# Retention and window-attention trunk: who makes the low parts of four sums of y in the recurrent blocks

## Chip, cores, metric

The kernel runs on one core of a Trainium2 chip. The metric is the device time of one execution in microseconds; lower is better. Times given as "median" are over several executions, times in the trace are those of one profiled execution.

## The reference

Input `x` is 2048 tokens by 1024 features, all in float32. Two layers and a norm:

```python
def reference(x, ...):
    h = x
    h = h + retention_layer(rmsnorm(h, ret_norm), ret_w_in, ret_w_out)   # 4 heads, q/k 256, v 512
    kb, vb = shared_kv(h, kv_norm, w_kv)                                 # once, banded
    h = h + swa_sink_layer(rmsnorm(h, swa_norm), swa_w_in, sinks, swa_w_out, kb, vb)
    return rmsnorm(h, final_norm)
```

What matters here is the end of a retention head: `y = o * silu(g)`, 512 tokens by 512 features for each block of tokens and head, times that head's 512 rows of `w_out`, added to the residual stream `h`.

## The kernel before

**Staging.** The 2048 tokens go through in 4 blocks of 512. Each block has four retention heads one after the other, then the window-attention layer ("post"). Five engines run programs of their own that meet at semaphores; each engine takes its instructions in the order in which the program lists them for it. An instruction whose `wait_ge` isn't fulfilled holds everything behind it on its engine. The five are TensorE (PE; its weight loads are listed as PEld), VectorE (DVE), ScalarE (ACT), GpSimd (POOL) and SyncE (SP), which issues nearly all transfers.

**High and low parts.** Every operand of a large matmul is split into a rounded high part (type fp32r) and the remainder, the low part. A product is three matmuls: high by high, high by low, low by high (`three`, L709 to L711). ScalarE makes most high parts, and the low part is `value - high` on another engine.

**The recurrent blocks.** Block 0 uses plain products. In the blocks 1, 2 and 3 the output product of a head, `y @ w_out`, is done by seven half-size products (a Strassen-Winograd scheme). `y` is transposed on TensorE into PSUM as four quarters A11, A12, A21, A22; four sums are made of them: S1 = A21 + A22, S2 = S1 - A11, S3 = A11 - A21, S4 = A12 - S2. The seven left operands are A11, A12, A22, S1, S2, S3, S4. Each product is 12 matmuls of 128x512.

**Two sorts of head.** Heads of block 1 (`one_head`, "slow heads" below) also prepare weight sums for the later blocks. For this GpSimd makes six pieces a head (`comb_piece(at, j)`, j from 0 to 5): four subtractions of raw weights in place (L655) when the raw data have landed, and a rounding (L663) that waits until the low part of the piece before is done. VectorE makes the piece's low part (`comb_less_hi`, L1979). Heads of the blocks 2 and 3 (`fast_head`, "fast heads") use these sums, and GpSimd has little to do in them. There are 4 slow heads and 8 fast ones.

**The end of a head.** TensorE does the products in this order: A22, the last transposes of y (four in a slow head, eight in a fast one), S1, A11, S2, S3, A12, S4. Before each product it waits for its low part (`part_wait`): for the four sums on the semaphore `s_parts_lo`, for the other three on `a_lo`. Products reuse PSUM banks: the S2 product (slow head) needs the A22 product added to `h`, and the S3 product needs `h_add` at 3, which is the two additions behind the S1 product.

ScalarE makes the high parts in the order A22, S1, A11, A12, S3, S2, S4 (`part_hi`, L1406 fast, L1533 slow). GpSimd makes the low parts of the sums in the order S1, S3, S2, S4 (`y_sums_lo`, L676), each as soon as the high part is there. VectorE, before and after:

```python
gate_y(1)                        # L1825 fast, L2096 slow: y = o * silu(g), last quarter
dve.wait_ge(p_mm.sem, at(p_mm, 1))   # the A22 product is done (t4_mm in a fast head)
add_product(2, 2, 0, 1)          # L1852 fast, L2144 slow: adds it to h
y_sum(S3)                        # L1842 fast, L2131 slow; waits for A12's high part
part_lo(A11)                     # L1678
y_sum(S2)
part_lo(A12)
y_sum(S4)
```

Then come, in a slow head, the low part of weight piece 4 (L1979), a wait for the S1 product, and two additions (`add_product`, L2144 or L1852). Behind these, `add_sum` (L1857, L2149) and `grow_sum` (L1861, L2153) take the other products in, each behind the product that it reads. In a slow head piece 5's low part (L1979 again) follows at the very end of the head.

In GpSimd's queue of a slow head, `y_sums_lo` stands between `comb_piece(at, 4)` and `comb_piece(at, 5)`. In the last head of block 1, TensorE goes on with the transposes of `h` (L1134), which wait for nearly all additions to `h`.

Of the kernel before, what the change touches and what calls it, by code (L numbers as in the profile page):

```python
# [32 lines left out]
F32 = mybir.dt.float32  # L33
F32R = mybir.dt.float32r
I32 = mybir.dt.int32
ALU = mybir.AluOpType
# [6 lines left out]
BLOCKS = SEQ // BT  # L43
# [23 lines left out]
A11, A12, A22, S1, S2, S3, S4 = range(7)  # L67
HI_ORDER = (A22, S1, A11, A12, S3, S2, S4)
LO_ORDER = (A22, A11, A12)
SUM_ORDER = (S1, S3, S2, S4)  # L70
# [38 lines left out]
def build(nc, x, x_t, stream, rope_a, rope_b, mask, ident, ret_cols, gains, sinks, fnorm, out):  # L109
    with ExitStack() as ctx:  # L110
# [89 lines left out]
        asum = {k: v.rearrange("p (t n) -> p t n", t=2) for k, v in asum.items()}  # L200
# [388 lines left out]
        def _(pool):  # L589
# [79 lines left out]
                    pool.wait_ge(x_part_hi.sem, at(x_part_hi, n + 1))  # L669
                    pool.tensor_tensor(xpart[a][1], xsum[a], xpart[a][0].bitcast(F32), ALU.subtract).then_inc(x_part_lo.sem, 1)  # L670

            def y_sums_lo(at):

                for n, a in enumerate(SUM_ORDER):
                    pool.wait_ge(a_hi.sem, at(a_hi, HI_ORDER.index(a) + 1))
                    pool.tensor_tensor(ahl[a][1], asum[a], ahl[a][0].bitcast(F32), ALU.subtract).then_inc(s_parts_lo.sem, 1)  # L676

            for b in range(1, BLOCKS - 1):
                for h in range(HEADS):
                    at = Place("head", b, h)  # L680
                    if b < FAST:
                        for j in range(4):
                            comb_piece(at, j)
                    elif h == 0:
                        x_sums_lo(b)
                    o_root(at)
                    if b < FAST:
                        comb_piece(at, 4)
                    y_sums_lo(at)
                    if b < FAST:  # L690
                        comb_piece(at, 5)
                h_root(Place("post", b), 1)
                h_root(Place("post", b), 2)
            x_sums_lo(BLOCKS - 1)
            for h in range(HEADS):
                o_root(Place("head", BLOCKS - 1, h))
                y_sums_lo(Place("head", BLOCKS - 1, h))
            at = Place("post", BLOCKS - 1)
            h_root(at, 1)
            for t in range(TT):  # L700
# [974 lines left out]
        def _(dve):  # L1675
            def less_hi(dst, src, hi, c):

                return dve.tensor_tensor(dst, src, hi.bitcast(F32), ALU.subtract).then_inc(c.sem, 1)  # L1678
# [78 lines left out]
            def one_block(b, first, last, combine=False):  # L1757
                w_used, w_ready = ring(b)

                def fast_head(h):  # L1760
# [66 lines left out]
                    def y_sum(a):  # L1827

                        done = lambda k: dve.wait_ge(a_sum.sem, at(a_sum, SUM_ORDER.index(k) + 1))
                        if a == S1:  # L1830
                            dve.wait_ge(a21_copied.sem, at(a21_copied, 1))
                            x0, x1, op = asum[S3], y_part(A22), ALU.add
                        elif a == S3:
                            dve.wait_ge(a_hi.sem, at(a_hi, HI_ORDER.index(A12) + 1))
                            x0, x1, op = y_part(A11), asum[S3], ALU.subtract
                        elif a == S2:
                            done(S1)
                            x0, x1, op = asum[S1], y_part(A11), ALU.subtract
                        else:
                            done(S2)  # L1840
                            x0, x1, op = y_part(A12), asum[S2], ALU.subtract
                        dve.tensor_tensor(asum[a], x0, x1, op).then_inc(a_sum.sem, 1)  # L1842

                    def part_lo(a):

                        dve.wait_ge(a_hi.sem, at(a_hi, HI_ORDER.index(a) + 1))
                        less_hi(ahl[a][1], y_part(a), ahl[a][0], a_lo)

                    def add_product(bank, rows, n, step):

                        cols = hres[:, rows:rows + 2, n * 512:(n + 1) * 512]
                        dve.tensor_tensor(cols, cols, ps[:, bank:bank + 2, :], ALU.add).then_inc(h_add.sem, step)  # L1852
# [13 lines left out]
                    def halves_done(n):  # L1866
                        dve.wait_ge(half_used.sem, at(half_used, n))
# [77 lines left out]
                    dve.wait_ge(x_loaded.sem, at(x_loaded, 0))  # L1945
                    dve.wait_ge(t4_mm.sem, at(t4_mm, 1))
                    add_product(0, 2, 0, 1)
                    y_sum(S3)
                    part_lo(A11)
                    y_sum(S2)  # L1950
                    part_lo(A12)
                    y_sum(S4)
                    halves_done(19)
                    add_product(2, 2, 1, 1)
                    add_product(2, 0, 1, 1)
# [27 lines left out]
                def one_head(h, seam=False, closing=False):  # L1983
# [133 lines left out]
                    def y_sum(a):  # L2117

                        done = lambda k: dve.wait_ge(a_sum.sem, at(a_sum, SUM_ORDER.index(k) + 1))
                        if a == S1:  # L2120
                            x0, x1, op = asum[S3], y_part(A22), ALU.add
                        elif a == S3:
                            dve.wait_ge(a_hi.sem, at(a_hi, HI_ORDER.index(A12) + 1))
                            x0, x1, op = y_part(A11), asum[S3], ALU.subtract
                        elif a == S2:
                            done(S1)
                            x0, x1, op = asum[S1], y_part(A11), ALU.subtract
                        else:
                            done(S2)
                            x0, x1, op = y_part(A12), asum[S2], ALU.subtract  # L2130
                        dve.tensor_tensor(asum[a], x0, x1, op).then_inc(a_sum.sem, 1)  # L2131

                    def part_lo(a):

                        if a == A22:
                            dve.wait_ge(a21_copied.sem, at(a21_copied, 1))
                        else:
                            dve.wait_ge(a_hi.sem, at(a_hi, HI_ORDER.index(a) + 1))
                        less_hi(ahl[a][1], asum[a] if a in asum else y_part(a), ahl[a][0], a_lo)

                    def add_product(bank, rows, n, step):

                        cols = hres[:, rows:rows + 2, n * 512:(n + 1) * 512]
                        dve.tensor_tensor(cols, cols, ps[:, bank:bank + 2, :], ALU.add).then_inc(h_add.sem, step)  # L2144
# [13 lines left out]
                    if first:  # L2158
                        gate_y(0)
                        gate_y(1)  # L2160
                        split_yt(0)
                        gate_y(2)
                        split_yt(1)
                        gate_y(3)
                        split_yt(2)
                        add_to_h(0, 0)
                        split_yt(3)
                        if first:
                            split_chunk(n0 + 7)
                        add_to_h(0, 1)  # L2170
                        add_to_h(0, 2)
                        add_to_h(0, 3)
                        if first:
                            split_chunk(n0 + 8)
                        for t in range(TT):
                            add_to_h(1, t)
                    else:
                        gate_y(2)
                        gate_y(3)
                        gate_y(0)  # L2180
                        part_lo(A22)
                        y_sum(S1)
                        gate_y(1)
                        dve.wait_ge(p_mm.sem, at(p_mm, 1))
                        add_product(2, 2, 0, 1)
                        y_sum(S3)
                        part_lo(A11)
                        y_sum(S2)
                        part_lo(A12)
                        y_sum(S4)  # L2190
                        if combine:
                            comb_less_hi(at, 4)
                        dve.wait_ge(p_mm.sem, at(p_mm, 2))
                        add_product(0, 2, 1, 1)
                        add_product(0, 0, 1, 1)
                        dve.wait_ge(p1_copied.sem, at(p1_copied, 1))
                        add_sum(0, 0, 0, 1)
                        dve.wait_ge(p_mm.sem, at(p_mm, 3))
                        grow_sum(0, 2, 2)
                        added(6)  # L2200
                        add_sum(1, 0, 1, 1)
                        dve.wait_ge(p_mm.sem, at(p_mm, 4))
                        grow_sum(1, 0, 1)
                        added(8)
                        add_sum(0, 2, 0, 2)
                        add_sum(0, 2, 1, 2)
                        dve.wait_ge(w_used.sem, at(w_used, 8))
                        add_product(6, 0, 0, 2)
                        dve.wait_ge(p_mm.sem, at(p_mm, 5))
                        add_product(4, 0, 1, 2)  # L2210
                        if combine and not closing:
                            comb_less_hi(at, 5)
# [304 lines left out]
```

## Time and profile before

| | |
|---|---|
| median of 3 runs | 2438.07 us (2436.65 to 2438.33) |
| the profiled execution | 2439.43 us, span 2437.6 us |
| TensorE (PE) busy | 2390.0 us, 98% |
| VectorE (DVE) busy | 1503.8 us, 62% |
| ScalarE (ACT) busy | 680.0 us, 28% |
| GpSimd (POOL) busy | 454.4 us, 19% |
| block 1 (600 to 1070 us), DMA busy | 0.97 |
| blocks 2 and 3 (1250 to 1660, 1840 to 2240), DMA busy | 0.80 |

The span runs from the first to the last instruction of the profiled execution. Starts in the rows are microseconds from the span's start. In rows of the order of time, the second number is how long the instruction took (several merged ones together, "x3"), and a bracket gives how long the engine sat idle before it and what ended this.

### The profile page before, as it was taken

To read this page: it belongs to the slowest core of one execution; us is meant where nothing else is said; L and a number is where in the kernel's file an instruction comes from. 1 tells how busy PE (TensorE), PEld (TensorE's weight loads), DVE (VectorE), ACT (ScalarE), POOL (GpSimd) and SP (SyncE) were. 2 spreads that over 40 slices of the span, in tenths; PEclk is the share of its full clock that TensorE was granted. 3 is DMA by queue.
4 is the path that set the end of the run, shared out by engine and by line. 5 is a ranking of instruction groups with operands and counts; after the bars stand their busy time and mean duration, and the time that the engine had idled before them with its cause. 6 is when DMAs were issued, how large, how long until landed. Compare 5 with 4: busy or idle time off the path is not lost.

```text
span 2437.6 us, 28654 instructions
## 1 busy us (share of the span) xinstructions
PE 2390.0 (98%) x11216; PEld 1964.5 (81%) x11216; DVE 1503.8 (62%) x2042; ACT 680.0 (28%) x1470; POOL 454.4 (19%) x322
## 2 busy tenths in 40 slices
PE   7999999999999999999999999999999999999998
PEld 6888888877887787878888888888888787888886
DVE  6554655567766777763767564565567745647384
ACT  2312212235221212232533121232352212313243
POOL 2111111221345665640010010100001101101000
PEclk9999999999999999999999999999999999999999
DMA  8667575654899999974379877775357977786433
GB/s 354 264 242 287 195 275 207 256 192 165 320 402 378 363 372 356 364 298 173 104 253 324 278 257 254 266 248 207 122 198 243 330 257 266 248 289 238 173 104 147
DMA packets 131834, 625.85 MB, mean 257 GB/s; under 512 B 8864, under 2 KB 9632, under 8 KB 109728
## 3 DMA queue, kind: packets, MB, share of 16 engines
q1 hardware_dynamic: 122864, 588.53, 66.8%
q10 hardware_dynamic: 8880, 36.18, 4.0%
q8 instruction: 49, 0.80, 0.1%
q14 instruction: 41, 0.34, 0.0%
HBM read 471.58 MB, written 153.09 MB: 256 GB/s over the span
## 4 chain that ended last, share of the span: by engine, by line
PE 90%; DVE 7%; issue 1%; DMA 1%; ACT 1%; POOL 0%; DVEq 0%; SPq 0%; POOLq 0%; ACTq 0%
PE ps L709 29%; PE ps L711 28%; PE ps L710 28%; PE ps L1219 2%; DVE ff L2288 1%; PE ps L1229 1%; DVE fr L1678 1%; PE ps L1027 1%; PE ps L857 1%; DVE mx L2328 1%; DMA whl<-comb_w 1%; DVE xlo L1678 0%; DVE ff L2358 0%; DMA raw<-in_stream 0%; PE ps L1159 0%
## 5 line engine op out<-in xcount | busy, mean ns | idle before, releaser
L709 PE MATMUL ps<-whl,xhi 128*128 128x512 f32 (+1 forms) x1088 | 416.7, 383 | 2.3 <-DVE xlo L1678 2.3
L711 PE MATMUL ps<-whl,xlo 128*128 128x512 f32 (+1 forms) x1088 | 411.5, 378 | 0.0
L710 PE MATMUL ps<-whl,xhi 128*128 128x512 f32 (+1 forms) x1088 | 410.4, 377 | 0.0
L709 PE MATMUL ps<-xhi,whl 128*128 128x512 f32 x768 | 303.8, 396 | 17.6 <-DVE xlo L1682 16.2
L711 PE MATMUL ps<-xhi,whl 128*128 128x512 f32 x768 | 300.2, 391 | 0.0
L710 PE MATMUL ps<-xlo,whl 128*128 128x512 f32 x768 | 299.5, 390 | 0.0
L709 PE MATMUL ps<-whl,fr 128*128 128x512 f32 x640 | 256.9, 401 | 5.6 <-DMA whl<-comb_w 3.2
L711 PE MATMUL ps<-whl,fr 128*128 128x512 f32 x640 | 254.5, 398 | 0.0
L710 PE MATMUL ps<-whl,fr 128*128 128x512 f32 x640 | 254.0, 397 | 0.0
L709 PEld LDWEIGHTS ps<-whl,xhi 128*128 128x128 f32 x1088 | 204.9, 188 | 40.1 <-issue 3.1
L711 PEld LDWEIGHTS ps<-whl,xlo 128*128 128x128 f32 x1088 | 204.7, 188 | 38.6
L710 PEld LDWEIGHTS ps<-whl,xhi 128*128 128x128 f32 x1088 | 205.0, 188 | 36.1
L709 PE MATMUL ps<-fr 128*128 128x512 f32 (+1 forms) x496 | 182.0, 367 | 4.8 <-DVE hres L2144 3.6
L655 POOL TENSOR_TENSOR raw<-raw 128x512 f32<-128x512 f32 x96 | 165.7, 1726 | 98.9 <-DMA raw<-in_stream 93.3
L709 PEld LDWEIGHTS ps<-xhi,whl 128*128 128x128 f32 x768 | 144.6, 188 | 46.7 <-issue 17.8
L710 PE MATMUL ps<-fr 128*128 128x512 f32 (+1 forms) x496 | 179.6, 362 | 0.0
L711 PE MATMUL ps<-fr 128*128 128x512 f32 (+1 forms) x496 | 179.5, 362 | 0.0
L711 PEld LDWEIGHTS ps<-xhi,whl 128*128 128x128 f32 x768 | 144.4, 188 | 30.9
L710 PEld LDWEIGHTS ps<-xlo,whl 128*128 128x128 f32 x768 | 144.8, 189 | 29.2
L709 PEld LDWEIGHTS ps<-whl,fr 128*128 128x128 f32 x640 | 120.7, 189 | 36.3 <-DVE hres L2144 3.7
L711 PEld LDWEIGHTS ps<-whl,fr 128*128 128x128 f32 x640 | 120.9, 189 | 29.0
L710 PEld LDWEIGHTS ps<-whl,fr 128*128 128x128 f32 x640 | 120.8, 189 | 27.5
(214 smaller groups left out, 3854.0 us busy)
## 6 DMA issues: line engine op xcount, KB each, us to landing
whl<-split_w SPq DMA_DIRECT2D x60, 2048.0 KB, 8.2
whl<-split_w SPq DMA_DIRECT2D x118, 1024.0 KB, 6.9
split_w<-whl SPq DMA_DIRECT2D x44, 2048.0 KB, 7.2
whl<-vg_w SPq DMA_DIRECT2D x64, 1024.0 KB, 6.9
raw<-in_stream SPq DMA_DIRECT2D x44, 1024.0 KB, 9.4
vg_w<-ff SPq DMA_DIRECT2D x32, 1024.0 KB, 10.3
whl<-comb_w SPq DMA_DIRECT2D x32, 1024.0 KB, 6.5
raw<-in_stream SPq DMA_DIRECT2D x50, 512.0 KB, 10.4
```

The lines of the kernel that those rows point to most:

```text
L655: pool.tensor_tensor(dst, plus, minus, ALU.subtract).then_inc(comb_sum.sem, 1)
L709: pe.matmul(dst, lhs[0], rhs[0], start=start, stop=False)
L710: pe.matmul(dst, lhs[0], rhs[1], start=False, stop=False)
L711: return pe.matmul(dst, lhs[1], rhs[0], start=False, stop=stop)
L857: tr = pe.transpose(ps[:, 4 + t, e * P:(e + 1) * P], on[:, t, e * P:(e + 1) * P], idt[:, :])
L1027: tr = pe.transpose(ps[:, 4 + t, e * P:(e + 1) * P], on[:, t, e * P:(e + 1) * P], idt[:, :])
L1219: mm = pe.matmul(ps[:, 4 + s % 2, r * 256:(r + 1) * 256], qt[:, i, n, 2 * r:2 * r + 2, :].rearrange("p f c -> p (f c)"), kwin[:, :, n // 2 ...
L1229: tr = pe.transpose(ps[:, 6, j * P:(j + 1) * P], probs[:, s % 2, j, :], idt[:, :])
L1678: return dve.tensor_tensor(dst, src, hi.bitcast(F32), ALU.subtract).then_inc(c.sem, 1)
L2288: dve.tensor_tensor(dst.rearrange("p (g c) -> p g c", c=32), src, cosb[:, a, t * 32:(t + 1) * 32].unsqueeze(1).broadcast_to([P, 16, 32]), ...
L2328: dve.tensor_reduce(mx[:, :], src, AX_X, ALU.max).then_inc(mx_done.sem, 1)
```

## The change

The four low parts leave GpSimd's queue and enter VectorE's: S1's directly behind the addition of the A22 product, those of S3, S2 and S4 behind the sum S4. It is done in both sorts of head (block 1's `one_head`, and `fast_head`), with the same values. The semaphore `s_parts_lo` counts as before, and TensorE's program is the same.

```diff
-            def y_sums_lo(at):
-
-                for n, a in enumerate(SUM_ORDER):
-                    pool.wait_ge(a_hi.sem, at(a_hi, HI_ORDER.index(a) + 1))
-                    pool.tensor_tensor(ahl[a][1], asum[a], ahl[a][0].bitcast(F32), ALU.subtract).then_inc(s_parts_lo.sem, 1)
...
                     if b < FAST:
                         comb_piece(at, 4)
-                    y_sums_lo(at)
                     if b < FAST:
                         comb_piece(at, 5)
...
+                    def sum_lo(a):
+
+                        dve.wait_ge(a_hi.sem, at(a_hi, HI_ORDER.index(a) + 1))
+                        less_hi(ahl[a][1], asum[a], ahl[a][0], s_parts_lo)
...
                     dve.wait_ge(t4_mm.sem, at(t4_mm, 1))
                     add_product(0, 2, 0, 1)
+                    sum_lo(S1)
                     y_sum(S3)
                     part_lo(A11)
                     y_sum(S2)
                     part_lo(A12)
                     y_sum(S4)
+                    sum_lo(S3)
+                    sum_lo(S2)
+                    sum_lo(S4)
                     halves_done(19)
...
                         dve.wait_ge(p_mm.sem, at(p_mm, 1))
                         add_product(2, 2, 0, 1)
+                        sum_lo(S1)
                         y_sum(S3)
                         part_lo(A11)
                         y_sum(S2)
                         part_lo(A12)
                         y_sum(S4)
+                        sum_lo(S3)
+                        sum_lo(S2)
+                        sum_lo(S4)
                         if combine:
                             comb_less_hi(at, 4)
```

## Rows read from the trace of the kernel before

**Rows 1.** The page, part 4: the chain that ended last, by engine.

```profile
PE 90%; DVE 7%; issue 1%; DMA 1%; ACT 1%; POOL 0%; DVEq 0%; SPq 0%; POOLq 0%; ACTq 0%
```

**Rows 2.** All instructions of L676 (start, then who waited for it).

```profile
L676 POOL TENSOR_TENSOR fr<-ff,fr x48: 1278/1300/3355, 726.3 to 2230.5; 128x512 fp32r<-128x512 f32 x48
...
  PEld ps L709: 2.2, 8
```

**Rows 3.** Order of time, fast head (block 2, head 2): start, us, engine, line.

```profile
1540.19 1.28 POOL L676 TENSOR_TENSOR fr<-ff,fr 128x512 fp32r<-128x512 f32 x1 [9.30 <-ACT fr L1406]
...
1540.72 1.22 DVE L1852 TENSOR_TENSOR hres<-hres,ps 128x1024 f32<-128x1024 f32 x1 [0.68 <-PE ps L711]
1541.52 0.19 PEld L709 LDWEIGHTS ps<-whl,fr 128*128 128x128 f32 x1 [0.27 <-POOL fr L676]
```

**Rows 4.** Order of time, slow head (block 1, head 2), at S1.

```profile
941.53 1.30 POOL L676 TENSOR_TENSOR fr<-ff,fr 128x512 fp32r<-128x512 f32 x1 [4.98 <-ACT fr L1533]
...
944.17 1.22 DVE L2144 TENSOR_TENSOR hres<-hres,ps 128x1024 f32<-128x1024 f32 x1 [0.80 <-PE ps L711]
944.30 0.19 PEld L709 LDWEIGHTS ps<-whl,fr 128*128 128x128 f32 x1
```

**Rows 5.** Order of time, VectorE, the same fast head.

```profile
1542.65 0.69 DVE L1842 TENSOR_TENSOR ff<-ps,ff 128x512 f32<-128x512 f32 x1 [0.70 <-ACT fr L1406]
...
1545.05 0.68 DVE L1842 TENSOR_TENSOR ff<-ps,ff 128x512 f32<-128x512 f32 x1
1545.65 2.34 DVE L1852 TENSOR_TENSOR hres<-hres,ps 128x1024 f32<-128x1024 f32 x2
```

**Rows 6.** Order of time, ScalarE, the same fast head.

```profile
1545.76 0.64 ACT L1406 ACTIVATE fr<-ff 128x512 fp32r<-128x512 f32 x1 [0.57 <-DVE ff L1842]
```

**Rows 7.** Order of time, VectorE, the same slow head.

```profile
945.72 0.69 DVE L2131 TENSOR_TENSOR ff<-ps,ff 128x512 f32<-128x512 f32 x1 [0.33 <-ACT fr L1533]
...
948.72 3.14 DVE L1979 TENSOR_TENSOR ff<-raw,ff 128x2048 fp32r<-128x2048 f32 x1
951.79 2.34 DVE L2144 TENSOR_TENSOR hres<-hres,ps 128x1024 f32<-128x1024 f32 x2
...
964.59 2.28 DVE L1979 TENSOR_TENSOR ff<-raw,ff 128x2048 fp32r<-128x2048 f32 x1
```

**Rows 8.** Order of time, TensorE, the same slow head, at S3.

```profile
954.18 0.50 PE L709 MATMUL ps<-fr 128*128 128x512 f32 x1 [1.21 <-DVE hres L2144]
```

**Rows 9.** GpSimd, then VectorE, earlier and later in the same slow head.

```profile
934.65 1.90 POOL L663 TENSOR_SCALAR ff<-raw 128x2048 fp32r<-128x2048 f32 x1
...
952.98 8.34 POOL L655 TENSOR_TENSOR raw<-raw 128x512 f32<-128x512 f32 x4
...
935.40 1.68 DVE L2096 TENSOR_TENSOR ff<-ff 128x512 f32<-128x512 f32 x1 [1.99 <-ACT ff L1524]
938.59 0.69 DVE L2096 TENSOR_TENSOR ff<-ff 128x512 f32<-128x512 f32 x1 [1.51 <-ACT ff L1524]
```

**Rows 10.** DMA queue and transfers of the raw data for piece 5, same head.

```profile
931.96 1.03 SPq L468 DMA_DIRECT2D raw<-in_stream  x2
...
raw<-in_stream SPq DMA_DIRECT2D x2, 512.0 KB, 11.4
```

**Rows 11.** Windows (third number from the end: granted clock); the TensorE waits before them.

```profile
589.30:592.70 3.40, 3.40 (x10) 2.61 (x9) 2.23 (x5) 2.07 (x11) 0.00 (x0) 0.50 0.93 390
...
739.40:742.80 3.40, 3.40 (x9) 2.64 (x9) 0.79 (x2) 0.00 (x0) 3.24 (x3) 0.51 1.08 452
...
588.36 0.50 PE L709 MATMUL ps<-whl,fr 128*128 128x512 f32 x1 [2.08 <-DVE whl L1720]
...
738.18 0.49 PE L709 MATMUL ps<-whl,fr 128*128 128x512 f32 x1 [3.25 <-DMA whl<-comb_w]
```

**Rows 12.** VectorE, then TensorE, at the end of block 1.

```profile
1064.90 5.20 DVE L2149 TENSOR_TENSOR hres<-hres,ff 128x1024 f32<-128x1024 f32 x2
...
1071.28 1.96 PE L1134 MATMUL ps<-idt,hres 128*128 128x128 f32 x16 [2.54 <-DVE hres L2144]
```

More of the change, by code:

```diff
@@ L696, in _ @@
                 o_root(Place("head", BLOCKS - 1, h))
-                y_sums_lo(Place("head", BLOCKS - 1, h))
             at = Place("post", BLOCKS - 1)
@@ L2131, in y_sum, with sum_lo @@
                         dve.tensor_tensor(asum[a], x0, x1, op).then_inc(a_sum.sem, 1)
+                    def sum_lo(a):
+                        dve.wait_ge(a_hi.sem, at(a_hi, HI_ORDER.index(a) + 1))
+                        less_hi(ahl[a][1], asum[a], ahl[a][0], s_parts_lo)
                     def part_lo(a):
```

## The prediction

> **What bounds the kernel now.** I read the page first. The chain that ended last is 90% TensorE, with VectorE a further 7% [rows 1]. So the change is worth what it does to the start of some matmul, and nothing else. The group of the moved operation comes next: 48 low parts on GpSimd, and in 8 of the 12 heads a TensorE weight load waited for one of them, 2.2 us in all [rows 2]. It is thus already on TensorE's path in the fast heads, by a hair. The third view is the order of time around the S1 product in both sorts of head. The question there: when is TensorE ready for the S1 product, when is S1's low part ready now, and when would VectorE have it?
>
> In a fast head (eight of them, four in each of the blocks 2 and 3) the A22 product is followed by eight transposes alone, and then TensorE wants S1. GpSimd made its low part from 1540.19 to 1541.47; the weights went in at 1541.52, after a wait of 0.27 us. VectorE meanwhile waited for the A22 product and began to add it at 1540.72 [rows 3]. TensorE was thus ready at 1541.25. In a slow head (block 1, four heads) it is the same with four transposes: low part ready at 942.83, TensorE at S1 at 944.30 without a wait, and VectorE's addition begins at 944.17 [rows 4].
>
> **What the change does at S1.** The new low part stands on VectorE's queue behind the addition, and the addition waits for the end of the very product that TensorE does just before S1. So between TensorE's end of A22 and its start of S1 there now lie one addition and one subtraction of VectorE, where only transposes lay.
>
> Fast head: the addition takes its place for 1.12 us (two in a row take 2.34, one alone 1.22 [rows 3, 5]), so the low part begins at about 1541.85. A 128x512 subtraction there takes 0.68 to 0.69 us, with 0.60 from start to start [rows 5]; that is of one PSUM operand, the new one has both in SBUF, and in the slow head such a one (L2096) takes 0.69 too when GpSimd stands idle [rows 9]. Ready at 1542.54, and TensorE starts some 0.05 later, as it does now after GpSimd: 1542.59 against 1541.52, or 1.07 us later. Bounds: 1.0 if the operations overlap as much as any in these rows, 1.2 if they don't overlap at all. The ScalarE high part that it needs was there, or GpSimd could not have begun at 1540.19.
>
> Is the 1.07 given back in the head? VectorE's next sum, S3, waited until 1542.65 for a high part anyway [rows 5], so S1's low part fills a gap of 0.70 and delays it by nothing. The other three low parts come behind S4's sum: 3 x 0.60 = 1.80. ScalarE's last high part is ready at 1546.40 and S4's low part comes up at 1546.85, so no wait [rows 5, 6]. The two additions move from 1545.65 to 1547.45 and end at 1549.8. TensorE needs them at its S3 product, three products behind S1; in the slow head three products take 8.67 us (944.30 to 952.97, where its wait begins [rows 4, 8]), so S3 is due at 1551.3. That is hidden, with 1.5 us left; without that cover, each low part would cost 0.60. A11's and S2's parts are ready at 1543.95 and 1546.95, before 1545.4 and 1548.3. After that VectorE waits for TensorE as before and the shift stays. TensorE's next head needs nothing that would absorb it. Eight heads: 8 x 1.07 = **+8.6 us** (8.0 to 9.6).
>
> **The slow heads.** Here VectorE is already late: TensorE waits 1.21 us at S3, until two additions (begun 951.79) have freed its banks [rows 7, 8]. So not S1 but VectorE's chain from 944.17 to 954.13 counts. S1's low part starts at 945.30 and would push S3's sum from 945.72 to 945.90, by 0.2. The three others add 1.8. Against this, L1979 (piece 4 of the weight sums) took 3.14 while GpSimd made low parts, and 2.28 without GpSimd [rows 7]. With the low parts gone GpSimd can have done the sums of piece 5 by then (its raw data, issued from 931.96 on, land after 11.4 us, at 943.4 or soon after [rows 10]) and must wait for L1979 itself before its next step. That gives back 0.86. Together 0.2 + 1.8 - 0.86 = +1.14.
>
> But GpSimd's piece 5 then runs from about 944 to 951 (its four sums took 8.34 us beside VectorE [rows 9]), just where VectorE makes low parts. An operation of VectorE with both operands in SBUF (L2096) took 1.68 beside GpSimd's L663 and ended 0.53 after it, as if it had let it pass first; with GpSimd idle it took 0.69 [rows 9]: up to 0.99 each. Between none of the four and all four (+4.0) I take a little under one, +0.78, as the first surely meets GpSimd and the last ones hardly. Behind these rows stands a rule of the Trainium skill ("GPSIMD Engine Reference", section "Key points"): GpSimd shares its SBUF interfaces with VectorE and contends with VectorE's instructions that have two SBUF inputs. By that rule alone every low part that overlaps would be priced at the upper end; by the rows only those are that meet it, and where GpSimd is idle, in the fast heads, none is.
>
> So the gate at S3 moves by +1.9 (0.9 to 5). S1 itself starts at 946.0 (945.30 + 0.69 + 0.05) to 947.0 (with 0.99 more) in place of 944.3; S2, which ended at 952.97, then ends at 955.7 at the latest, before the gate at 954.18 + 1.9 = 956.1, so this delay is contained in the gate's. Heads 1 and 2 pay this in full: **+3.8**. Head 0 has a wait of 3.25 us for a transfer ahead of its S2 product, and right after it the granted clock is 0.51 for 3.4 us [rows 11]. Any delay before goes into that wait; S3 now starts about when that slow stretch ends, at 742.4 or so (738.18 + 2.8 for twelve matmuls + 1.7 lost at half clock, less a little), and VectorE's additions would end near 741. If the wait, now split in two, no longer brings the clock down, the head gains up to 1.4; if it does, 0. I take **-0.7**. Head 3 ends in a wait of 2.54 us for VectorE, whose two additions took 5.20 beside GpSimd's piece 5 [rows 12] against 2.34 for two of this size elsewhere [rows 5]: with GpSimd done, VectorE ends near 1070.3 and TensorE, 1.9 later, frees itself at 1070.6, against 1071.28: **-0.65**.
>
> The sum: 8.6 + 3.8 - 0.7 - 0.65 = **+11.1 us**. Against the profiled execution's 2439.43 (span 2437.6) this makes 2450.5; its time lies 1.4 over the median 2438.07 of the three runs shown, to which the forecast refers: **2449.2 us**, 0.45% slower. A measurement of this kernel can tell some 0.2%, 4.9 us, from no change.
>
> **The rivals.**
> *Clock.* The new waits might bring TensorE's clock down. For: it fell to about 0.5 for 3.4 us behind head 0's wait of 3.25, and behind one of 2.08 in block 0 [rows 11], each fall costing half of 3.4, 1.7 us. Against: the wait of 1.21 in the slow head and one of 2.54 at block 1's end had matmuls at full speed on both sides [rows 8, 12], and the fast heads' new wait is 1.34 (1541.25 to 1542.59). A fall in each of three slow heads: +5, so 2454; in all eight fast heads too, +13.6 more. Chance 0.17.
> *Collision in block 1.* GpSimd meets all four low parts and L1979 stays at 3.14: the gate moves by 0.2 + 1.8 + 4.0 = 6.0 in three heads instead of 1.9, head 3's gain is gone: 2438.1 + 8.6 + 18 = 2464; half of it 2456. Chance 0.10.
> *Block 1 gives it all back.* GpSimd out of the way of L1979 and of the additions behind it (3.14 to 2.28, 5.20 to 2.34). It decides if all of the 0.86 + 2.86 were on TensorE's path in three heads, -11: then 2438 or so. Against: behind S3 VectorE waits for TensorE. Chance 0.05.
> *Faster (the other side).* The low part of S1 takes 0.69 on VectorE against 1.28 on GpSimd; ready earlier by the difference, it would end the eight waits of 2.2 us in all: 2436. It decides from a low part ready before 1541.25, so begun before the addition; VectorE sits idle for 0.68 there [rows 3], but its queue has the addition first. Chance 0.03. (The skill's same section holds VectorE to be about twice as fast at elementwise work; the rows agree, 0.69 against 1.28.)
> *Forecast.* 2445 to 2454: chance 0.65.
>
> Range: 2444 to 2457, so as to hold the clock's cases in the slow heads and half of the collision's. Faster 0.03; within 0.2% 0.07 (the third rival's 0.05, and 0.02 of the forecast below its edge); slower 0.90.
>
> **What would show it.** In each fast head a wait of TensorE of about 1.3 us for VectorE's new line (0.27 for GpSimd before), eight times; heads 1.07 longer; no wait at S3. In slow heads a wait at S1 of 1.7 to 2.7 for the same line, and one at S3 for L2144, its start 1.9 later after S1's old time; L1979 of piece 4 at 2.28; GpSimd's L655 of piece 5 from 944. Head 0 without a clock fall. I am wrong if a fast head is not longer, or if VectorE's additions in it end after TensorE is due at S3.

## The result and the profile after

| | median | runs | against before, 95% interval |
|---|---|---|---|
| before | 2438.2 us | 4 (2436.65 to 2439.09) | |
| changed | 2457.4 us | 4 (2456.71 to 2458.32) | 1.0079 (1.0066 to 1.0091) |

The change costs 19.2 us where +11 was forecast, and 2457.4 lies just above the range's 2457. Run again later beside its parts, it took 2455.45 us against 2437.75, 1.0074 (1.0061 to 1.0088): +17.7, and inside the range. Which side of the edge it falls on is scatter; that the cost is well above 11 is not: both intervals begin at 15 us or more.

The page of the changed kernel. Its chain has more VectorE in it than before [rows 1], and GpSimd's group of 48 low parts is gone; VectorE's L1670 is the line of `less_hi` now. Other lines that moved: TensorE's L709 to L711 are L701 to L703; VectorE's L1842 and L2131 (sums) are L1834 and L2132, L1852 and L2144 (additions) L1849 and L2150, L1979 is L1980.

```profile
span 2454.9 us, 28662 instructions
...
PE 89%; DVE 8%; issue 2%; DMA 1%; ACT 0%; POOL 0%; DVEq 0%; SPq 0%; ACTq 0%; POOLq 0%
```

All waits of TensorE that came from the change, by line. The 13 waits for L1670 (a low part) are the eight of the fast heads, four at S1 in the slow heads and one at S2; the three for L2150 (the additions before S3) are in heads 0 to 2 of block 1. Before there were 3.6 us for the additions and nothing for a low part, apart from the 2.2 us of weight loads for GpSimd [rows 2]. Two old waits shrink in turn: head 0's for a transfer from 3.25 to 1.07, and the 2.54 at the end of block 1 is gone.

```profile
PE ps L701 <- DVE fr L1670: 15.8, 13, 2.2
PE ps L701 <- DVE hres L2150: 7.3, 3, 2.8
```

**Where the time went.** Two small operations of GpSimd mark the progress of the work: L631 stands once in every head, and the L609 shown here at the start and at the end of block 1's heads, then at the end of those of blocks 2 and 3. Their starts, before:

```profile
643.39 1.02 POOL L609 TENSOR_TENSOR rstd<-ms,mhalf 128x4 f32<-128x4 f32 x1 [23.44 <-DVE ms L1687]
...
710.15 1.02 POOL L631 TENSOR_TENSOR ors<-ov,mhalf 128x4 f32<-128x4 f32 x1 [5.25 <-DVE ov L2085]
...
819.90 1.02 POOL L631 TENSOR_TENSOR ors<-ov,mhalf 128x4 f32<-128x4 f32 x1 [6.97 <-DVE ov L2085]
...
925.70 1.02 POOL L631 TENSOR_TENSOR ors<-ov,mhalf 128x4 f32<-128x4 f32 x1 [7.20 <-DVE ov L2085]
...
1031.37 1.02 POOL L631 TENSOR_TENSOR ors<-ov,mhalf 128x4 f32<-128x4 f32 x1 [6.90 <-DVE ov L2085]
...
1080.41 2.99 POOL L609 TENSOR_TENSOR rstd<-ms,mhalf 128x4 f32<-128x4 f32 x1 [11.39 <-DVE ms L1687]
...
1667.38 1.01 POOL L609 TENSOR_TENSOR rstd<-ms,mhalf 128x4 f32<-128x4 f32 x1 [19.58 <-DVE ms L1687]
...
2251.38 1.01 POOL L609 TENSOR_TENSOR rstd<-ms,mhalf 128x4 f32<-128x4 f32 x1 [19.60 <-DVE ms L1687]
```

and after:

```profile
643.74 1.02 POOL L609 TENSOR_TENSOR rstd<-ms,mhalf 128x4 f32<-128x4 f32 x1 [23.44 <-DVE ms L1679]
...
710.81 1.02 POOL L631 TENSOR_TENSOR ors<-ov,mhalf 128x4 f32<-128x4 f32 x1 [5.25 <-DVE ov L2086]
...
821.43 1.02 POOL L631 TENSOR_TENSOR ors<-ov,mhalf 128x4 f32<-128x4 f32 x1 [6.86 <-DVE ov L2086]
...
930.62 1.02 POOL L631 TENSOR_TENSOR ors<-ov,mhalf 128x4 f32<-128x4 f32 x1 [7.26 <-DVE ov L2086]
...
1039.38 1.02 POOL L631 TENSOR_TENSOR ors<-ov,mhalf 128x4 f32<-128x4 f32 x1 [6.89 <-DVE ov L2086]
...
1088.28 3.00 POOL L609 TENSOR_TENSOR rstd<-ms,mhalf 128x4 f32<-128x4 f32 x1 [17.44 <-DVE ms L1679]
...
1680.17 1.01 POOL L609 TENSOR_TENSOR rstd<-ms,mhalf 128x4 f32<-128x4 f32 x1 [37.71 <-DVE ms L1679]
...
2268.65 1.01 POOL L609 TENSOR_TENSOR rstd<-ms,mhalf 128x4 f32<-128x4 f32 x1 [37.15 <-DVE ms L1679]
```

The differences of these starts make the ledger. Block 1, from its 643.39 to 1080.41, took 437.0 us and now takes 444.5: **+7.5**, by heads +0.9, +3.4, +3.1 and -0.1, with 0.3 before the first. Blocks 2 and 3 (to 2251.38, with the window-attention layers between) took 1171.0 and now 1180.4: **+9.4** in eight heads.

**A fast head**, block 2, head 2, in order of time (TensorE's weight loads among it), to be held against [rows 3, 5]:

```profile
1551.34 1.22 DVE L1849 TENSOR_TENSOR hres<-hres,ps 128x1024 f32<-128x1024 f32 x1 [0.70 <-PE ps L703]
...
1552.48 0.69 DVE L1670 TENSOR_TENSOR fr<-ff,fr 128x512 fp32r<-128x512 f32 x1
1553.22 0.19 PEld L701 LDWEIGHTS ps<-whl,fr 128*128 128x128 f32 x1 [1.35 <-DVE fr L1670]
1553.22 0.50 PE L701 MATMUL ps<-whl,fr 128*128 128x512 f32 x1 [1.11 <-DVE fr L1670]
...
1556.26 1.88 DVE L1670 TENSOR_TENSOR fr<-ff,fr 128x512 fp32r<-128x512 f32 x3
1558.07 2.34 DVE L1849 TENSOR_TENSOR hres<-hres,ps 128x1024 f32<-128x1024 f32 x2
```

The addition (L1849) begins when A22 is done, S1's low part (L1670) 1.14 later, and TensorE's weight load has waited 1.35 for it. The last three low parts take 1.88 together and the two additions begin behind them; TensorE doesn't wait for them.

**A slow head**, block 1, head 2: VectorE, then GpSimd, then TensorE, against [rows 7, 8]:

```profile
949.12 1.22 DVE L2150 TENSOR_TENSOR hres<-hres,ps 128x1024 f32<-128x1024 f32 x1 [1.34 <-PE ps L703]
950.26 0.68 DVE L1670 TENSOR_TENSOR fr<-ff,fr 128x512 fp32r<-128x512 f32 x1
950.86 0.68 DVE L2132 TENSOR_TENSOR ff<-ps,ff 128x512 f32<-128x512 f32 x1
...
953.85 3.85 DVE L1670 TENSOR_TENSOR fr<-ff,fr 128x512 fp32r<-128x512 f32 x3
957.62 2.28 DVE L1980 TENSOR_TENSOR ff<-raw,ff 128x2048 fp32r<-128x2048 f32 x1
959.83 2.34 DVE L2150 TENSOR_TENSOR hres<-hres,ps 128x1024 f32<-128x1024 f32 x2
...
950.40 6.15 POOL L655 TENSOR_TENSOR raw<-raw 128x512 f32<-128x512 f32 x4 [8.90 <-DMA raw<-in_stream]
960.09 1.90 POOL L663 TENSOR_SCALAR ff<-raw 128x2048 fp32r<-128x2048 f32 x1 [3.54 <-DVE ff L1980]
...
951.00 0.51 PE L701 MATMUL ps<-whl,fr 128*128 128x512 f32 x1 [1.47 <-DVE fr L1670]
...
957.23 0.49 PE L701 MATMUL ps<-whl,fr 128*128 128x512 f32 x1 [0.36 <-DVE fr L1670]
...
962.22 0.50 PE L701 MATMUL ps<-fr 128*128 128x512 f32 x1 [1.93 <-DVE hres L2150]
```

The first low part takes 0.68, but the three behind S4's sum take 3.85 instead of some 1.9: GpSimd's four L655 of piece 5 run from 950.40 to 956.55 beside them. What VectorE does between, five sums and parts with one operand in PSUM, keeps its 0.68 beside GpSimd (950.86). In these rows only operations that have both operands in SBUF, and that begin while GpSimd is at work, are held up. TensorE waits three times, 1.47 for S1's low part, 0.36 for S2's, and 1.93 for the additions. L1980, piece 4's low part, is at 2.28 as forecast.

**Head 3 of block 1**, TensorE, and windows with the granted clock as the third number from the end:

```profile
1060.69 0.80 PE L701 MATMUL ps<-whl,fr 128*128 128x512 f32 x1 [2.16 <-DVE fr L1670]
...
1056.90:1060.30 3.40, 1.63 (x10) 1.14 (x8) 2.17 (x2) 1.09 (x2) 1.40 (x2) 1.00 1.06 416
1060.30:1063.70 3.40, 3.01 (x7) 2.43 (x8) 3.40 (x7) 1.30 (x3) 3.24 (x3) 0.54 1.03 398
1063.70:1067.10 3.40, 3.40 (x15) 2.69 (x15) 3.40 (x4) 0.59 (x1) 0.80 (x1) 0.96 0.97 389
```

Here GpSimd did meet S1's low part, which took 1.37, TensorE waited 2.16, and the granted clock fell to 0.54 for the next 3.4 us, which is nearly all of them at the lower of its two levels (1.2 of 2.4 GHz). Head 0's fall [rows 11] is gone in turn.

### The profile page after: what moved, and what is told of

The parts are those of the page before. It is cut to its first block, busy times and chain, and to the rows that moved or that the text cites. A ratio compares the mean times of both kernels' runs of the same rounds, so it can differ in the third digit from the quotient of the medians.

```text
span 2454.9 us, 28662 instructions
## 1 busy us (share of the span) xinstructions
PE 2391.9 (97%) x11216; PEld 1964.6 (80%) x11216; DVE 1535.7 (63%) x2090; ACT 680.6 (28%) x1470; POOL 373.7 (15%) x274
## 4 chain that ended last, share of the span: by engine, by line
PE 89%; DVE 8%; issue 2%; DMA 1%; ACT 0%; POOL 0%; DVEq 0%; SPq 0%; ACTq 0%; POOLq 0%
PE ps L701 28%; PE ps L703 28%; PE ps L702 28%; PE ps L1211 2%; DVE fr L1670 1%; DVE ff L2298 1%; PE ps L1221 1%; DVE mx L2338 1%; PE ps L849 1%; DVE hres L1849 0%; DVE hres L2150 0%; DVE xlo L1670 0%; DMA raw<-in_stream 0%; DMA comb_w<-ff 0%; DVE ff L2368 0%
## 5 line engine op out<-in xcount | busy, mean ns | idle before, releaser
L701 PE MATMUL ps<-whl,xhi 128*128 128x512 f32 (+1 forms) x1088 | 416.7, 383 | 2.8 <-DVE xlo L1670 2.8
L703 PE MATMUL ps<-whl,xlo 128*128 128x512 f32 (+1 forms) x1088 | 411.6, 378 | 0.0
L701 PE MATMUL ps<-xhi,whl 128*128 128x512 f32 x768 | 303.8, 396 | 17.8 <-DVE xlo L1674 16.4
L703 PE MATMUL ps<-xhi,whl 128*128 128x512 f32 x768 | 300.3, 391 | 0.0
L701 PE MATMUL ps<-whl,fr 128*128 128x512 f32 x640 | 258.2, 403 | 19.0 <-DVE fr L1670 15.8
L703 PE MATMUL ps<-whl,fr 128*128 128x512 f32 x640 | 254.2, 397 | 0.0
L701 PEld LDWEIGHTS ps<-whl,xhi 128*128 128x128 f32 x1088 | 204.9, 188 | 40.6 <-issue 3.6
L703 PEld LDWEIGHTS ps<-whl,xlo 128*128 128x128 f32 x1088 | 204.7, 188 | 38.8
L701 PE MATMUL ps<-fr 128*128 128x512 f32 (+1 forms) x496 | 182.1, 367 | 8.5 <-DVE hres L2150 7.3
L655 POOL TENSOR_TENSOR raw<-raw 128x512 f32<-128x512 f32 x96 | 158.2, 1648 | 166.1 <-DMA raw<-in_stream 160.4
L701 PEld LDWEIGHTS ps<-xhi,whl 128*128 128x128 f32 x768 | 144.6, 188 | 47.0 <-issue 18.0
L703 PE MATMUL ps<-fr 128*128 128x512 f32 (+1 forms) x496 | 179.6, 362 | 0.0
L703 PEld LDWEIGHTS ps<-xhi,whl 128*128 128x128 f32 x768 | 144.4, 188 | 30.9
L701 PEld LDWEIGHTS ps<-whl,fr 128*128 128x128 f32 x640 | 120.9, 189 | 50.2 <-DVE fr L1670 18.4
L1670 DVE TENSOR_TENSOR fr<-ff,fr 128x512 fp32r<-128x512 f32 (+1 forms) x128 | 117.1, 943 | 53.5 <-ACT fr L1405 10.1
L703 PEld LDWEIGHTS ps<-whl,fr 128*128 128x128 f32 x640 | 120.9, 189 | 29.7
```

The lines of the kernel that those rows point to most:

```text
L655: pool.tensor_tensor(dst, plus, minus, ALU.subtract).then_inc(comb_sum.sem, 1)
L701: pe.matmul(dst, lhs[0], rhs[0], start=start, stop=False)
L703: return pe.matmul(dst, lhs[1], rhs[0], start=False, stop=stop)
```

## The experiments

My theory after the result: (a) in the fast heads S1's place behind the addition is the whole cost, 1.1 each; (b) in the slow heads the three low parts in VectorE's chain to the S3 product cost, and more than their own time, since GpSimd's piece 5 meets them. Rivals: VectorE's added load (48 operations) costs wherever it is; S1's wait with the clock falls is the slow heads' cost too.

The parts first, each on its own. "Slow only" and "fast only" keep GpSimd's `y_sums_lo` in the other sort of head, where VectorE's four `sum_lo` are left out. (Shortened: the call alone, `y_sums_lo` now being given its list of sums.)

```diff
# fast only: the change in fast_head, GpSimd keeps all four in block 1; slow only: the other way round
-                    y_sums_lo(at)
+                    y_sums_lo(at, SUM_ORDER if b < FAST else ())     # fast only
+                    y_sums_lo(at, () if b < FAST else SUM_ORDER)     # slow only
```

> The change in the eight fast heads alone; block 1 as before. Queue theory (the low part of S1 stands behind the A22 addition, and nothing else in these heads costs): the changed kernel's fast heads are 1.1 us longer each, so +8.9 us, about 2447. Rival, VectorE's load (each of the new low parts costs where VectorE is near the path, the last three too): more than +8.9, up to 8 x 2.9 = +23. Rival, clock: a fall of TensorE's clock in some heads, 1.7 us each, on top of +8.9.

> The change in block 1 alone; the fast heads as before. Queue and collision with GpSimd's piece 5: by the changed kernel's profile +0.9 in head 0, +3.4 and +3.1 in heads 1 and 2, about 0 in head 3 with a clock fall in it: +7.5 to +10, about 2447. With the fast heads alone it should add up to the change's +19. Rival (the forecast's own sizes, 0.78 for the collision): +2.5.

Fast only: 2446.29 us, +7.9 over 2438.42; its heads in block 1 as before and +8.9 in blocks 2 and 3 by the starts (table below). Slow only: 2447.26, +8.8; block 1 +6.5, blocks 2 and 3 +0.6. The parts make 16.7, against the 17.7 and 19.2 of the whole. Neither part is the cause alone. The interval of each ratio in this section is 0.0012 to 0.0014 to either side, some 3 us, for runs of five or six executions, and 0.0009, 2.2 us, for those of eleven.

**S1 before the addition**, all else as in the change:

```diff
                     gate_y(1)
+                    sum_lo(S1)
                     dve.wait_ge(x_loaded.sem, at(x_loaded, 0))
                     dve.wait_ge(t4_mm.sem, at(t4_mm, 1))
                     add_product(0, 2, 0, 1)
-                    sum_lo(S1)
```

(and the same in the slow head.)

> The change, but S1's low part stands before the A22 addition in VectorE's queue, in all heads; all four low parts are still VectorE's. Queue theory: no wait of TensorE at S1, the fast heads 0.2 shorter than before; in block 1 the last three low parts still meet GpSimd's piece 5 and hold the S3 product: +3 in heads 1 and 2, +1 in head 0, no clock fall in head 3: in all +4 to +6, about 2443. Rival, VectorE's load (48 more operations, 33 us of work): it stays at +15 or more, since the load is the same.

2448.21 us, +9.8. The load rival's +15 is off; my +4 to +6 is too little as well. Blocks 2 and 3 are at +0.7 where I expected them below the kernel before, and block 1 is at +7.6. The fast heads' rest has a place. TensorE's weight load for S2, in a head of block 2, idle time in brackets:

```profile
1554.63 0.19 PEld L701 LDWEIGHTS ps<-whl,fr 128*128 128x128 f32 x1 [0.31 <-DVE fr L1670]
```

With S1 on time, S2's low part is the next that is late, by 0.31: in VectorE's queue it stands behind S4's sum and behind the low part of S3, although TensorE wants S2 before S3. (With the two exchanged nothing was run.) In block 1, head 2, the waits of TensorE are 1.1 for a low part and 1.9 for the additions, as in the table of waits:

```profile
PE ps L701 <- DVE hres L2150: 1.9, 1, 1.9
PE ps L701 <- DVE fr L1670: 1.1, 1, 1.1
```

Block 1 loses as much without any wait at S1, but this is partly chance: the clock falls in three heads here and in one of the change (table below). Where it doesn't fall, in head 1, the S3 product begins 2.1 later after L631 than before, and 3.4 later in the change. That a wait of 1.48 at S1 is by itself nearly contained in the one at S3 is shown by "S1 late alone" below: TensorE has it in heads 1 and 2 and doesn't wait at S3, and they are 0.3 and 0.6 longer.

**GpSimd's piece 5 late**, with the change otherwise:

```diff
                     if b < FAST:
+                        pool.wait_ge(comb_lo.sem, at(comb_lo, 5))
                         comb_piece(at, 5)
```

> The change, but GpSimd begins piece 5 only when VectorE has made the low part of piece 4, so it stands still beside the four low parts and beside L1979. Collision theory: the last three low parts take 1.9 in place of 3.8, S1's never 1.4, no clock fall in head 3: slow heads 1 and 2 at +1.1 each, fast heads as in the change: +11 to +13, about 2450. Rival (they are slow for a reason of their own, operands in SBUF or ScalarE's high parts): they stay at 3.8 and the time at 2457.

2449.36 us, +10.9, against the rival's 2457. VectorE in block 1, head 2, and GpSimd's piece 5:

```profile
948.33 1.88 DVE L1671 TENSOR_TENSOR fr<-ff,fr 128x512 fp32r<-128x512 f32 x3
950.13 2.28 DVE L1981 TENSOR_TENSOR ff<-raw,ff 128x2048 fp32r<-128x2048 f32 x1
952.33 2.34 DVE L2151 TENSOR_TENSOR hres<-hres,ps 128x1024 f32<-128x1024 f32 x2
...
959.85 4.06 DVE L2156 TENSOR_TENSOR hres<-hres,ff 128x1024 f32<-128x1024 f32 x2
...
952.50 7.28 POOL L655 TENSOR_TENSOR raw<-raw 128x512 f32<-128x512 f32 x4 [17.02 <-DVE ff L1981]
```

The three low parts take 1.88. The collision moves to the additions at 959.85, 4.06 for two beside GpSimd's rounding (L663, from 959.87 to 962.85); in this head nobody waits for them. At the end of block 1 TensorE waits 1.8 for VectorE, which the change had done away with. Block 1 is at +1.7 instead of +6.5 to +7.5, with the wait at S1 still in it, and its heads 1 and 2 at +1.1 and +1.7. One wait on GpSimd, which adds nothing to anyone's work, gives back 7 to 8 of the 18 to 19 us, and 4.8 to 5.8 of it lie in block 1 by the starts. The collision is shown. The profile has no clock fall in block 1 either, so the 4.8 to 5.8 hold the one or two falls of the change, 1.7 each, as well; the rest lies where the edit changes nothing, and no run says why.

**One low part or three**, of the four:

(Shortened: the calls of `y_sums_lo` alone.)

```diff
# S1 early alone / S1 late alone: GpSimd keeps the three others
+                    y_sums_lo(at, SUM_ORDER[1:])
# three alone: GpSimd keeps S1's, on a semaphore of its own; S3, S2 and S4 stand on VectorE as in the change
+                    y_sums_lo(at, SUM_ORDER[:1])
```

> Only S1's low part moves to VectorE, and stands before the A22 addition; the other three stay GpSimd's, in all heads. Queue theory: no wait of TensorE at S1, nothing else changed: -2 to +1 us, about 2438. Rival, VectorE's load: 12 more operations, +2 or more.

> Only S1's low part moves, and stands behind the A22 addition as in the change; the other three stay GpSimd's. Queue theory: the fast heads +8.8 in all, the slow heads +0.2 to +0.7 each, since their S3 product is held by VectorE's chain anyway: +9 to +11, about 2448. Rival (the last three low parts are what costs in the fast heads): near 0 there.

> Only the low parts of S3, S2 and S4 move to VectorE, behind S4's sum; S1's stays GpSimd's (with a semaphore of its own). Queue and collision theory: fast heads unchanged, block 1 like that of the kernel with S1 early: waits of about 1.1 at S2 and 1.9 at S3 in heads 1 to 3 and clock falls behind some of them: +6 to +8, about 2445. Rival (S1's place is what costs in block 1 too): near 0.

> The changed kernel as it is, on the same chip as the parts above: +19, and close to the sum of S1 late alone and of the three alone (+9 to +11 and +6 to +8) if the two costs are separate; clearly more than the sum if the two waits of a slow head together bring the clock down where one doesn't.

S1 early alone: 2435.65 (2437.75 before), 0.9993 (0.9984 to 1.0002). S1 late alone: 2446.24, +8.5, of it +8.8 in blocks 2 and 3, and block 1 is even 2.4 shorter. Three alone: 2447.63, +9.9, with +7.3 in block 1 and +0.6 in the others. The change beside them: +17.7. The sum of the late one and the three is 18.4, so by the medians the two costs are separate, and the surplus that two waits in one head might have brought isn't seen. By the starts it is less clean: in block 1 the two make 4.9, the change +6.5. Three alone cost more than my +6 to +8; its granted clock fell in three of the four heads.

**Both causes taken away**: S1 before the addition and piece 5 late (the two edits above together), all four low parts on VectorE.

> All four low parts on VectorE, with both causes taken away: S1's before the A22 addition, and GpSimd's piece 5 only behind the low part of piece 4. If the two causes are all: fast heads as in the kernel before, or 0.1 to 0.3 shorter each; heads 1 and 2 of block 1 +0.9 each for three low parts in the chain to S3, no clock fall: -2 to +2 us, about 2438. If the load on VectorE cost anything more: above +3.

2441.3 us, 1.0015 (1.0006 to 1.0024), +3.9. This is above the -2 to +2 that I expected, and above the +3 from which, as I had written, the load on VectorE costs something more. Its profile has block 1 at 437.05 and blocks 2 and 3 at 1170.9, both as before; the whole 2.0 us of its span over that of before lie ahead of block 1 (645.39 against 643.39), in code that the two share. In the other profiles this point lies between 642.93 and 644.67. The other 1.9 is that the profiled execution of before, 2439.43, lies 2.0 above the median 2437.43 of the runs beside this one. So against before, where the measured rest sits isn't settled.

Against "S1 early alone" it is clearer, and there the two causes are not all. The kernels differ in the three other low parts and piece 5's place, and in 6.0 us: 3.8 in block 1 and 2.3 in blocks 2 and 3. In the fast heads TensorE's weight load for S2 waits 0.3 eight times, as above. In block 1 heads 1 and 2 are 0.9 longer each, the chain to S3, and head 3 is 1.9 longer, with waits of 1.7 at S3 and 1.8 at the block's end in place of 1.1 and 0.9. So the low parts of S3, S2 and S4 cost on VectorE without any collision too; the result equals the kernel before because S1's low part, on VectorE and early, gives back about as much.

**VectorE's chain to S3 made shorter**: the low part of weight piece 4 goes behind the sum that takes S2 in, once in the best version so far (S1 early alone) and once in the change.

```diff
                         y_sum(S4)
-                        if combine:
-                            comb_less_hi(at, 4)
...
                         grow_sum(0, 2, 2)
+                        if combine:
+                            comb_less_hi(at, 4)
```

> A version meant to beat both: S1's low part alone on VectorE, before the A22 addition, and the low part of weight piece 4 (L1979) moved behind the sum that takes the S2 product in, so that it no longer stands before the two additions that the S3 product waits for. If that chain is what holds S3: the waits of 1.1 at S3 go in heads 1 and 2 (-2.2), nothing in head 3, where VectorE's end counts, on top of the -2.1 of the early low part alone: about 2433.5. Rival (piece 4 is then late for its store and for the next weights): 2437 or more.

> The change as it is, with the low part of weight piece 4 moved behind the sum that takes the S2 product in. If VectorE's chain to the S3 product is the slow heads' cost: no wait at S3 there, the wait at S1 of 1.5 and a small one at S2 stay, so +1.5 to +2.5 in heads 1 and 2; fast heads +8.8: about +12, 2450. If S1's wait and clock falls were the slow heads' cost: it stays at 2455.

In the change: 2449.97 us, +12.5, as expected; no product of block 1 waits for the additions any more, only the transposes at its end do (2.1), and block 1 is at +1.0. TensorE still waits for S1's low part in every head here, 1.48 and in head 2 2.34, and the clock doesn't fall. In the best version: 2436.18, 0.9994 (0.9985 to 1.0003), no gain over S1 early alone. Heads 1 and 2 are 1.4 shorter each, where the theory had 1.1, but at the end of block 1 TensorE waits 4.0 for VectorE, 2.54 before [rows 12], and the clock falls:

```profile
PE ps L1134 <- DVE hres L2155: 4.0, 1, 4.0
```

All of it in one table, in us: head 0, 1 and 2 of block 1 from one L631 to the next; head 3 from its L631 to L609; blocks 2 and 3 from L609 to L609; clock: mean granted clock of these four stretches, each 0.02 (0.03 in head 3) being one fall.

| kernel | head 0 | head 1 | head 2 | head 3 | clock | blocks 2, 3 | median, over before |
|---|---|---|---|---|---|---|---|
| before | 109.75 | 105.80 | 105.67 | 49.04 | .98 1 1 1 | 1171.0 | |
| changed | 110.62 | 109.19 | 108.76 | 48.90 | 1 1 1 .97 | 1180.4 | +19.2 |
| changed, again | 110.43 | 108.79 | 108.37 | 48.84 | 1 1 .98 .97 | 1180.1 | +17.7 |
| fast only | 108.88 | 105.84 | 105.94 | 49.09 | .98 1 1 1 | 1179.8 | +7.9 |
| slow only | 111.39 | 108.52 | 108.41 | 48.52 | .98 1 .98 1 | 1171.5 | +8.8 |
| S1 early | 110.60 | 107.87 | 109.32 | 49.90 | .98 1 .98 .97 | 1171.6 | +9.8 |
| piece 5 late | 107.25 | 106.92 | 107.41 | 49.40 | 1 1 1 1 | 1179.6 | +10.9 |
| S1 early alone | 107.57 | 105.84 | 105.66 | 47.35 | 1 1 1 1 | 1168.6 | -2.1 |
| S1 late alone | 107.33 | 106.13 | 106.22 | 47.52 | 1 1 1 1 | 1179.7 | +8.5 |
| three alone | 110.36 | 108.72 | 107.83 | 49.89 | .98 .98 1 .97 | 1171.6 | +9.9 |
| early, piece 5 late | 107.05 | 106.77 | 106.60 | 49.20 | 1 1 1 1 | 1170.9 | +3.9 |
| early alone, piece 4 behind | 107.52 | 104.38 | 104.22 | 50.46 | 1 1 1 .97 | 1168.3 | -1.3 |
| change, piece 4 behind | 107.80 | 106.38 | 106.80 | 49.48 | 1 1 1 1 | 1179.7 | +12.5 |

## Why the prediction was wrong

**The fast heads: right.** Forecast 8 x 1.07 = 8.6; the profiles have 8.6 to 9.4 wherever S1 stands behind the addition, and 0.7 or less wherever it doesn't. The new wait of the weight load was forecast as 1.34 and is 1.35 [rows 3]. The three other low parts cost nothing there as long as S1 is late (1179.7 with and 1180.4 or 1180.1 without them on GpSimd); the forecast's cover, 1.5 us to S3, held.

**The step that failed is the collision's size in the slow heads.** I put it at 0.78 a head, "the first surely meets GpSimd and the last ones hardly". My price of one meeting, up to 0.99, was about right; I had too few of them, under one a head. There are two in each slow head, in both profiles of the change. In head 2 the raw data, issued from 936.89, let GpSimd begin at 950.40, 13.5 later and not 11.4, just after S1's low part had begun; then it met the first two of the three others, and the last ran free, as GpSimd ended at 956.55:

```profile
953.85 1.54 DVE L1670 TENSOR_TENSOR fr<-ff,fr 128x512 fp32r<-128x512 f32 x1
955.32 1.78 DVE L1670 TENSOR_TENSOR fr<-ff,fr 128x512 fp32r<-128x512 f32 x1
957.02 0.68 DVE L1670 TENSOR_TENSOR fr<-ff,fr 128x512 fp32r<-128x512 f32 x1
```

Together that is 3.85 - 1.88 = 1.97. With it, the gate at S3 (the time from L631 to the start of the S3 product) moves by 0.2 + 1.8 + 1.97 - 0.86 = 3.1, and head 2 is 3.1 longer, head 1 3.4: 6.5 in place of 3.8. Which two are met depends on when the transfer lands: in the change's head 3, and in heads 1 to 3 of the same kernel run again, GpSimd began early enough to meet S1's low part (1.16 to 1.37 us) and then the first of the three (1.49 to 1.55), which costs 1.3 to 1.6 a head. The rival "collision in block 1" had the mechanism, at too high a price (all four met, while two were; and L1980 did fall to 2.28 there) and with a chance of 0.10 only. Piece 5 late puts heads 1 and 2 at +1.1 and +1.7, where the sum without a collision says +1.14.

**Head 0: wrong sign, -0.7 forecast and +0.9 measured.** The clock fall did go. But two low parts met GpSimd here too (4.12 for three), and so did L1980 (3.38), so that VectorE's additions, forecast to end near 741, ended at 744.0 and held S3 for 2.6:

```profile
734.32 4.12 DVE L1670 TENSOR_TENSOR fr<-ff,fr 128x512 fp32r<-128x512 f32 x3
738.37 3.38 DVE L1980 TENSOR_TENSOR ff<-raw,ff 128x2048 fp32r<-128x2048 f32 x1
741.67 2.34 DVE L2150 TENSOR_TENSOR hres<-hres,ps 128x1024 f32<-128x1024 f32 x2
...
744.06 0.49 PE L701 MATMUL ps<-fr 128*128 128x512 f32 x1 [2.60 <-DVE hres L2150]
```

With piece 5 late the head is 2.5 shorter than before: that gain exists and was eaten.

**Head 3: -0.65 forecast, -0.1 measured.** TensorE's wait at the end of the block is gone, as forecast; the clock fall behind the wait of 2.16 at S1 took most of what it gave. With S1's low part alone moved, head 3 is 1.5 to 1.7 shorter.

**The clock.** The rival's mechanism occurs: falls stand behind waits of 1.95 to 2.3 at S1, and in "S1 early" behind 1.1 and 1.9 within one head. It isn't regular: waits of 2.15 at S1 (the change again, head 1), of 2.20 ("slow only", head 1) and of 2.34 ("change, piece 4 behind", head 2), and of 2.6 and 2.8 at S3 in the change, brought no fall. Before and after have one fall each in block 1, so it isn't what makes the difference between these two. How often it falls from one execution to the next isn't shown, as each run has one profile.

**The sum.** 9.4 + 7.5 = 16.9 of the profile's 17.3 is placed. That the medians differ by 19.2 the first time and 17.7 the second is left to the scatter of executions: the profiled execution of before, 2439.43, is slower than all four in the result, and that of the change is the fastest of its four. Of the 8.1 us between forecast and median, 2.7 are in heads 1 and 2, 1.6 in head 0, 0.5 in head 3, 0.8 in the fast heads, 0.7 ahead of these heads, and 1.9 are this scatter.

## What to carry to other kernels

Before an operation is moved to another engine, write down what its new neighbour in the queue waits for: a part that the next product needs must not stand behind the addition of the last one. When the engine that is relieved has other work waiting, say when that work will now run and against what; here it was a transfer's landing that decided it, and a low part of 128x512 that met GpSimd's work took 1.16 to 1.79 in place of 0.68. Count the engine's order too: with no collision the three low parts still cost 6.0 us, the late piece 5 included, since they stand in VectorE's chain to S3, and S2's behind S3's. The version that beats the changed kernel is the move of S1's low part alone, ahead of the addition; against the kernel before, its 2.1 us are not shown to be a gain (0.9984 to 1.0002).

## What the runs showed that I had not expected

With TensorE's waits of 1.1 and 1.9 about 5 us apart in a head, the granted clock fell behind some of them and not behind others (table: heads 2 and 3 of "S1 early", not head 1). Two additions of 128x1024 with both operands in SBUF took 2.36 alone (before, from 746.92) and 4.06 beside GpSimd's rounding ("piece 5 late", from 959.85), so the collision isn't special to the small low parts. Removing only S1's low part from GpSimd shortened block 1 by 2.4 us with VectorE's part late and by 3.7 with it early, and heads 0 and 3 by 3.9 together in both; I had expected nothing there. Of the 2.2 to 2.4 in head 0, 1.7 is a clock fall that isn't there. Why was not tested: the transfer wait of 2.48 in "three alone" had a fall behind it, the ones of 2.53 in "S1 early alone" and 2.69 in "early alone, piece 4 behind" had none.
